# The second block's projection tiles split into high and low parts, and the feed forward's first two tiles multiplied behind its norm

## The reference, cut to what matters

```
h = rmsnorm(x) * (1 + scale) + shift
u = h @ w_in_2[l]                 # 1024 x 2560: 20 tiles of 128 columns
x_lru, gate, q, k, v = split(u)   # 4 tiles each
a = conv -> rg_lru(x_lru) * gelu(gate)
b = diff_attention(rope(q), rope(k), v), then a norm per head
x = x + g1 * (concat(a, b) @ w_out_2[l])
h = rmsnorm(x) * (1 + scale) + shift
x = x + g2 * (swiglu(h) in layer 0, eight routed experts in layer 1)
```

## Time and profile before

| what | us |
|---|---|
| median of 3 runs (2630.61 to 2631.39) | 2630.64 |
| the profiled execution's own time | 2629.47 |
| its span, first to last instruction | 2627.6 |
| TensorE busy | 2565.2 (98%) |
| VectorE busy | 1956.2 (74%) |
| ScalarE busy | 1407.4 (54%) |
| mean granted TensorE clock | 0.99 of full |

### The profile page before, as it was taken

One profiled execution on the slowest core, in us unless ns is written; L12 is line 12 of the kernel. 1 busy time (PEld: TensorE's weight loads), 2 busy tenths in 40 slices (PEclk: granted clock), 3 DMA queues, 4 the chain that ended last, 5 costly groups with the idle time before them and its releaser, 6 DMA issues. The chain is left out here.

```text
span 2627.6 us, 41652 instructions
## 1 busy us (share of the span) xinstructions
PE 2565.2 (98%) x14530; PEld 2221.3 (85%) x14530; DVE 1956.2 (74%) x2656; ACT 1407.4 (54%) x1803; POOL 0.2 (0%) x4
## 2 busy tenths in 40 slices
PE   9999999998999999999999999999999999999998
PEld 5798788897888888898788998878888888888887
DVE  6698358896788777776645654558989889898897
ACT  4653242384544444444434433447777677777775
POOL 0000000000000000000000000000000000000000
PEclk9999999999999999999999999999999999999999
DMA  9422335425788878785434564439999999999996
GB/s 357 149 89 97 128 112 146 148 81 180 241 305 294 297 277 278 257 288 190 140 99 121 183 184 151 138 141 366 352 355 350 349 354 358 350 362 338 365 350 225
DMA packets 223741, 627.11 MB, mean 239 GB/s; under 512 B 15344, under 2 KB 23568, under 8 KB 223376
## 3 DMA queue, kind: packets, MB, share of 16 engines
q1 hardware_dynamic: 223632, 625.64, 68.6%
HBM read 619.29 MB, written 6.29 MB: 238 GB/s over the span
## 5 line engine op out<-in xcount | busy, mean ns | idle before, releaser
L3396 DVE TENSOR_TENSOR wide_low<-wide,wide_high 128x2048 fp32r<-128x2048 f32 x288 | 657.1, 2289 | 98.1 <-ACT wide_high L3271 96.0
L3271 ACT ACTIVATE wide_high<-wide 128x2048 fp32r<-128x2048 f32 x288 | 552.4, 1919 | 197.2 <-PE bank L3124 128.5
L229 DVE TENSOR_TENSOR expert_tile_low<-slot,expert_tile_high 128x1024 fp32r<-128x1024 f32 x216 | 263.8, 1223 | 122.3 <-ACT expert_tile_high L221 118.5
L221 ACT ACTIVATE expert_tile_high<-slot 128x1024 fp32r<-128x1024 f32 x216 | 227.3, 1054 | 182.9 <-PE bank L238 62.7
L3120 PE MATMUL bank<-wide_high,xg_high 128*128 128x512 f32 x768 | 302.8, 394 | 1.2 <-DVE xg_low L3348 1.2
L3121 PE MATMUL bank<-wide_high,xg_low 128*128 128x512 f32 x768 | 299.5, 390 | 0.0
L3124 PE MATMUL bank<-wide_low,xg_high 128*128 128x512 f32 x768 | 205.6, 389 | 0.0
L237 PE MATMUL bank<-h_high,expert_tile_high 128*128 128x256 f32 x704 | 173.4, 284 | 0.0
L238 PE MATMUL bank<-h_low,expert_tile_high 128*128 128x256 f32 x704 | 172.6, 283 | 0.0
L1997 PE MATMUL bank<-expert_tile_high,act_hi 128*128 128x512 f32 x512 | 161.4, 397 | 11.1 <-DVE act_lo L2148 11.1
L3124 PEld LDWEIGHTS bank<-wide_low,xg_high 128*128 128x128 f32 x768 | 144.2, 188 | 30.3
(11 more groups left out here) (537 smaller groups left out, 5035.5 us busy)
## 6 DMA issues: line engine op xcount, KB each, us to landing
wide<-in_moe_gu SPq DMA_DIRECT2D x192, 1024.0 KB, 5.9
wide<-in_moe_d SPq DMA_DIRECT2D x96, 1024.0 KB, 6.2
slot<-in_peer_u SPq DMA_DIRECT2D x128, 512.0 KB, 4.4
slot<-in_peer_v SPq DMA_DIRECT2D x128, 512.0 KB, 4.5
slot<-in_w_in SPq DMA_DIRECT2D x72, 512.0 KB, 3.7
picked_or_ada<-in_ada_w SPq DMA_DIRECT2D x48, 512.0 KB, 5.0
ada_slot<-in_ada_w SPq DMA_DIRECT2D x48, 512.0 KB, 4.6
slot<-in_ffn_gu SPq DMA_DIRECT2D x48, 512.0 KB, 3.6
```

The lines of the kernel that those rows point to most:

```text
L221: core.nc.scalar.activation(self.tile_hi[:, place % 2], core.slot[u][:], ACT.Copy).then_inc(self.hi_ready.sem, 1)
L229: core.nc.vector.tensor_tensor(self.tile_lo[:, place % 2], slot[:], self.tile_hi[:, place % 2].bitcast(F32), ALU.subtract)\
L3271: nc.scalar.activation(w_hi[n % NB][:].rearrange("p c n -> p (c n)"), wide[n % U][:], ACT.Copy).then_inc(hi_ready.sem, 1)
L3396: nc.vector.tensor_tensor(w_lo[n % NB][:].rearrange("p c n -> p (c n)"), wide[n % U][:], w_hi[n % NB][:].rearrange("p c n -> p (c n)").bit ...
```

## The change

1. In both layers the tiles at places 8 to 11 (the middle queries and keys) and 16 to 19 (gelu), and in layer 1 also those at places 2 to 5, are multiplied split instead of whole: 8 tiles in layer 0, 12 in layer 1. The value tiles and the others stay whole.
2. The high parts are made on ScalarE just before `empty(n - 2)`, each waiting for its buffer (two buffers in turn: the high products and the low part of two split tiles earlier). The low parts are made on VectorE at fixed places of its list: tile 8 after the product of gate and convolution, 9 after `soften(0)`, 10 after the next step of the recurrence, 11 after `finish(0)`, 16 after `finish(2)`, 17 to 19 after `finish(3)`. TensorE waits in each split tile between its 16 high and its 8 low products for that low part.
3. The activations are split as well: eight small copies on ScalarE and eight subtractions on VectorE in each layer.
4. SP reloads a buffer as soon as its tile is split, not when it is multiplied.
5. In layer 0 the norm before the feed forward writes the high parts of `h` directly (ScalarE) and the low parts directly (VectorE, one per chunk, among its scalings), and the first two feed forward tiles, split during the output projection, are multiplied chunk by chunk behind it (`pair`). `feed_forward` begins with its third tile.
6. The norm's squares and the position tables use the room of `z` and `att` instead of tiles of their own.

The core of the diff (`...` where lines are left out):

```diff
+    EARLY_SPLIT, MIDDLE_SPLIT = [2, 3, 4, 5] if l == 1 else [], [8, 9, 10, 11]
+    HALVED = EARLY_SPLIT + MIDDLE_SPLIT + [n for n in range(T) if 4 <= ORDER[n] < 8]
...
             for n in range(4, T):
-                sp.wait_ge(used.sem, used.at(n - 3))
+                if n - 4 in HALVED:
+                    sp.wait_ge(low_made.sem, low_made.at(HALVED.index(n - 4) + 1))
...
+            def split_tile(k, out):
+                pe.wait_ge(halver.low_split.sem, halver.low_split.at(C))
+                pe.wait_ge(high_made.sem, high_made.at(k + 1))
+                for c in range(C):
+                    nc.tensor.matmul(out, tile_hi(k)[:, c, :], split.high[:, c, :], start=(c == 0), stop=False)
+                    last = nc.tensor.matmul(out, tile_hi(k)[:, c, :], split.low[:, c, :], start=False, stop=False)
+                last.then_inc(high_used.sem, 1)
+                pe.wait_ge(low_made.sem, low_made.at(k + 1))
+                for c in range(C):
+                    last = nc.tensor.matmul(out, tile_lo(k)[:, c, :], split.high[:, c, :], start=False, stop=(c == C - 1))
+                last.then_inc(used.sem, 1)
...
+            def pair():
+                for c in range(C):
+                    pe.wait_ge(halver.low_split.sem, halver.low_split.at(C + c + 1))
+                    for u in range(2):
...
+            def tile_high(k):
+                n = HALVED[k]
+                u = n % U
+                act.wait_ge(core.landed[u].sem, core.landed[u].at(16 * (n // U + 1)))
+                if previous(k) is not None:
+                    act.wait_ge(high_used.sem, high_used.at(previous(k) + 1))
+                    act.wait_ge(low_made.sem, low_made.at(previous(k) + 1))
+                nc.scalar.activation(tile_hi(k), core.slot[u][:], ACT.Copy).then_inc(high_made.sem, 1)
...
+            def tile_low(k):
+                dve.wait_ge(high_made.sem, high_made.at(k + 1))
+                if previous(k) is not None:
+                    dve.wait_ge(used.sem, used.at(HALVED[previous(k)] + 1))
+                nc.vector.tensor_tensor(tile_lo(k), core.slot[HALVED[k] % U][:], tile_hi(k).bitcast(F32), ALU.subtract).then_inc(low_made.sem, 1)
...
+            tile_lows(8)
             rope(1)
             soften(0)
+            tile_lows(9)
...
+            tile_lows(10)
             rope(2)
             soften(1)
             finish(0)
+            tile_lows(11)
             rope(3)
```

More of the change, by code:

```diff
@@ L2280, with __init__ @@
 class NormParts:
-    def __init__(self, core, ctx, name, x, out, gain, shift, bank):
+    def __init__(self, core, ctx, name, x, out, gain, shift, bank, room, halver=None, split=None, splits=0):
         self.core, self.x, self.out, self.gain, self.shift, self.var = core, x, out, gain, shift, bank[:, 0:N]
-        self.sq = core.sb(ctx, f"{name}_squares", [P, C, N])
+        self.halver, self.split, self.splits = halver, split, splits
+        self.sq = room[:, 0:C, :]
         self.std, self.rstd = (core.sb(ctx, f"{name}_{part}", [P, N]) for part in ("std", "rstd"))
@@ L2304, in vector, with low @@
                 .then_inc(self.scaled.sem, 1)
+            if self.split is not None and c >= 2:
+                self.low(dve, c - 2)
+        if self.split is not None:
+            self.low(dve, C - 2)
+            self.low(dve, C - 1)
+    def low(self, dve, c):
+        nc, split, halver = self.core.nc, self.split, self.halver
+        dve.wait_ge(self.scaled.sem, self.scaled.at(c + 1))
+        dve.wait_ge(halver.moving_split.sem, halver.moving_split.at(self.splits + c + 1))
+        nc.vector.scalar_tensor_tensor(split.low[:, c, :], self.out[:, c, :], self.shift[:, c:c + 1], split.high[:, c, :].bitcast(F32),
+                                       ALU.add, ALU.subtract).then_inc(halver.low_split.sem, 1)
     def squares(self, act, ready=None):
@@ L2516, in passed, with mix_layer @@
             count.passed(k)
-def mix_layer(core, ctx, a, l, x, mods, cos, sin, hide, lam, next_tiles, router):
+def mix_layer(core, ctx, a, l, x, mods, cos, sin, hide, lam, next_tiles, router, split, halver):
     nc = core.nc
@@ L2709, in _ @@
             idle_products(core, 1, 3)
+            if ahead:
+                for u in range(2):
+                    pe.wait_ge(halver.hi_ready.sem, halver.hi_ready.at(u + 1))
+                    pe.wait_ge(halver.lo_ready.sem, halver.lo_ready.at(u + 3))
+                pair()
             if router is not None:
@@ L2843, in _ @@
                 pos.vector(dve)
-            for t in range(T4):
-                convolve(t)
+            if EARLY_SPLIT:
+                activations_low()
+                tile_lows(2, 3)
+            convolve(0)
+            tile_lows(4)
+            convolve(1)
+            tile_lows(5)
+            convolve(2)
+            convolve(3)
             if l == 0:
                 opening.vector_late(dve)
+            if not EARLY_SPLIT:
+                activations_low()
             dve.wait_ge(gated.sem, gated.at(4))
@@ L2889, in _ @@
                                         core.col(f"subln_g{l}", 0), 1.0 - lambda_init(l), ALU.mult, ALU.mult).then_inc(heads_mixed.sem, 1)
+            if ahead:
+                for u in range(2):
+                    halver.lower(dve, u, 0)
             for t in range(C):
@@ L2939, in _, with gate_and_up @@
             zero_banks(core, pe, range(4, 8))
-            pe.wait_ge(halver.low_split.sem, halver.low_split.at(C))
-            with pe.Fori(0, R1) as i:
-                for u in range(U):
+            def gate_and_up(i, start):
+                for u in range(start, U):
                     if u % 2 == 0:
@@ L2958, in silu, with round_ @@
                 nc.scalar.activation(sg[:, w, :], core.bank[2 * w][:, 0:N], ACT.Silu).then_inc(silued.sem, 1)
-            def round_(place, i, before, here):
-                for u in range(U):
+            def round_(place, i, before, here, start=0):
+                for u in range(start, U):
                     halver.high(act, place + u, i)
@@ L3010, in feed_forward @@
     own.passed(FT)
-    halver.passed(U * R, True)
+    halver.passed(U * R, False)
     for u in range(U):
```

123 lines of the change are left out of this document (96 added, 27 removed).

## The result

| | median us | runs |
|---|---|---|
| before | 2630.64 | 5 (2628.24 to 2631.66) |
| after | 2641.98 | 5 (2640.53 to 2643.55) |

The ratio after to before is 1.0042, with a 95% interval of 1.0031 to 1.0053: slower by 11.3 us. The profiled execution of after took 2643.55 us, its span 2641.8.

A forecast was written before the change was run, and what follows sets the result against it. TensorE, busy for 98% of the span, was taken as the bound. Layer 0 +7.3, layer 1 +1.8, the feed forward's start -4.0 and the clock +8.5 gave +13.6 us: 2644 against the median, range 2635 to 2651.

The forecast's parts named there:

- The win per tile: Split tiles in both layers: 2.88 us instead of 3.45, winning 0.57 each, 4.6 in layer 0 and 6.8 in layer 1.
- low parts for places 2 to 5 of layer 1: Layer 1's first tiles: VectorE's added 8.2 us just fits; full 2.3 us win taken, bound 0 to 2 us late.
- The waits: TensorE waits for low parts: tile 8 (layer 0) 3.2 us, tile 9 2.8, tile 11 4.6, tile 16 0.9.
- Small delays on ScalarE: Exponentials and bank emptying behind new ScalarE waits: 0.4 us in layer 0, 0.3 in layer 1.
- The feed forward: From the norm to the third feed forward tile: -4.0 us, bounds -4.5 and -2.0; gap 1.6, clearing 3.4.
- The clock: Behind five new waits in the two layers the clock halves, 1.7 us each: +8.5 us, bounds 0 and 12.5.
- the bound of 1.7 us: Feed forward's start: if the clock falls in the remaining 1.6 us gap, up to 1.7 us goes back.
- Rival A: Same waits in both layers, but the clock holds: +5.1 us, 2636; chance 0.16.
- C: Clock stays low for 5 us each time and falls in the norm too: +19.3 us, 2650; chance 0.2.
- The sum: Whole kernel: +7.3 + 1.8 - 4.0 + 8.5 = +13.6 us, 2644 against the median; chance 0.57.
- Rival B: Low parts come in time in VectorE's list, so waits vanish: 15.4 us won, 2615; chance 0.07.

The follow-up runs named there:

- E2: The changed kernel with all late low parts (tiles 8 to 11, 16, 17) moved earlier in VectorE's list: 2617.95 us, ratio 0.9949 to before.
- E5: The changed kernel with zero matmuls between high and low products of tiles 9, 11 and layer 0's tile 8: 2634.93 us, one run.
- E3: The changed kernel with only tile 11's low part moved, from behind finish(0) to ahead of rope(2): 2631.81 us, one run.
- E6: The changed kernel with only tile 11's low part moved ahead of finish(0), still behind soften(1): 2640.14 us, one run.
- E8: The changed kernel with only tile 9's low part moved, from behind soften(0) to ahead of rope(1): 2637.91 us, one run.
- E4: The changed kernel with no layer tile split, only the feed forward's first two tiles multiplied behind the norm: 2627.79 us, ratio 0.9985 to before.
- E7: E2 with the feed forward's four banks cleared behind the norm's products, replacing idle products there: 2615.03 us, ratio 0.9934 to before.

## Why the prediction was right

**Direction and size.** 2644 was forecast, 2642.0 measured, inside the range, and by the mechanism of the forecast. That the total came so near is in part luck: the clock was put 3.9 us too high, and untouched code, forecast at 0, ran longer in these executions.

**The win per tile.** Without any wait (E2) 8 split tiles win 82.33 - 77.69 = 4.64 us and 12 win 82.33 - 75.39 = 6.94: 0.58 a tile, against 0.57. The rule of the Trainium skill (FP8 and Floating Point Precision, TensorE Precision Notes) on passes would have given an estimate of 0.86 a tile, 17 for 20 tiles; the runs show 11.6. VectorE's low parts for places 2 to 5 of layer 1, which just fitted by the forecast, did fit: no low product there waits.

**The waits.** E5 less E2 is what they cost at full clock: 89.17 - 77.69 = 11.48 in layer 0, forecast 11.5; 83.69 - 75.39 = 8.30 in layer 1, forecast 8.3. They came at the foreseen tiles and at no other. Each stands in the trace 0.3 us shorter than forecast (2.94 for 3.2, 2.5 for 2.8, 4.30 for 4.6, 0.60 for 0.9), because I counted from one start to the next, while the idle time counts from the modelled end of the last record, which is longer than a product's 0.12 us. From start to start layer 0's four are 3.22, 2.79, 4.58 and 0.88 us, 11.47 in all, and that is what the kernel pays. E3, E6 and E8 show the waits of tiles 9 and 11 to be the place in the list: the low part, moved ahead of the steps named as the cause, is no longer late. The low parts of tiles 8 and 16 were moved only together with all others, in E2, where their waits go too.

**Small delays on ScalarE.** I put them at 0.4 and 0.3. By the two sums above nothing is left for them.

**The feed forward.** -4.0 in after and -4.3 alone (E4), against -4.0. The gap was 2.00 us, not 1.6, and the clearing 3.1, not 3.4, so two errors cancelled. In E2 the clock did fall there, the case that the bound of 1.7 us was kept for.

**The clock.** The one term that was mis-sized: 8.5 forecast, 4.64 measured (E5). A fall costs 1.55, close to 1.7; but two of the five waits, tile 8's 2.94 us and layer 1's tile 9 with 2.52, had none behind them in the profiled run. I had taken the three waits of the earlier trace rows as proof that every wait of that size costs the clock. That was one execution's evidence, and two rows speak against it: the first is after's, behind the same L1631 wait of the earlier trace rows (2.82 us there), the second before's own, behind a shorter wait, 2.17 us at L1997, a line that led the list of waits and that the earlier trace rows leave out. The granted clock is 1.00 in both.

```profile
401.12:404.42 3.30, 3.30 (x29) 3.30 (x30) 1.46 (x7) 1.51 (x3) 0.00 (x0) 1.00 0.02 5
```

```profile
801.00:804.00 3.00, 3.00 (x16) 2.46 (x16) 3.00 (x4) 0.48 (x2) 0.00 (x0) 1.00 0.96 363
```

The L1631 wait, 2.7 to 2.9 us in all ten profiles, had a fall right behind it only in that of before. Rival A, no fall at all, was wrong as well, and so was C.

**The sum.** Forecast in full: +13.6. Measured in the touched stretches: +9.92 + 2.92 - 4.0 + 0.4, in all +9.3. Of the difference of 4.3, 3.9 is the clock and 0.7 the small delays, less the 0.4 between the layers, which I had at 0; the little that is left is rounding and the win per tile. The profiled run of after was nevertheless 14.1 us above that of before. The rest, 3.87 + 1.0 = 4.9, lies in untouched code. Of the 3.87, 2.49 are there by the first product of L1121, at 37.58 us in before and 40.07 in after. The clock of after fell 4.0 us earlier in this stretch: the same sixteen products took 1.95 us in before and 3.58 in after.

```profile
33.03 1.95 PE L1089 MATMUL bank<-strip_sum,mod_first_rows 128*128 128x2 f32 x16 [0.81 <-DVE mod_first_rows L970]
```

```profile
33.89 3.58 PE L1089 MATMUL bank<-strip_sum,mod_first_rows 128*128 128x2 f32 x16 [0.79 <-DVE mod_first_rows L970]
```

By the medians the change costs 11.3; what of the 2 us between this and 9.3 is spread of such falls no run here separates.

**Rival B** had asked for the low parts in time, 15.4 us won. I gave it 0.07, rightly for this list; E2, the same instructions in another order, won 12.7, and E7 16.0, with the clearing moved as well.

## What to carry to other kernels

When a second engine prepares an operand in a list of strict order, place that step by when the consumer needs it, ahead of steps that themselves hang on the consumer's newest output; VectorE was busy for only two thirds of these stretches, and that average could not show that TensorE would wait. Before deciding that a split isn't worth it, try it with the producer moved: here the same work went from 0.4% slower to 0.5% faster. Filling such a wait with idle matmuls brings back the clock, not the wait.

## What the runs showed of the hardware that had not been expected

Whether the clock falls behind a wait of 2 to 3 us isn't settled by the length of the wait. Layer 0's tile 8 waited 2.94, 2.94, 2.93 and 2.93 us in after, E3, E6 and E8. The rows of the stretch right behind it, in E3 and then in E8:

```profile
1309.30:1312.60 3.30, 3.30 (x12) 2.67 (x12) 0.34 (x1) 2.27 (x4) 0.00 (x0) 0.50 0.73 230
```

```profile
1309.30:1312.60 3.30, 3.28 (x21) 2.54 (x22) 2.82 (x4) 3.06 (x4) 0.00 (x0) 1.00 0.72 210
```

The same instructions, 12 matmuls in one and 21 in the other: E3 and E6 ran at 1.2 GHz there, 6.8 us in all, from 0.9 us before the wait ended, while after and E8 kept 2.4. In the same way layer 1's tile 9 waited 2.52 in three kernels: the clock held in after and E6 and fell in E3. The 2.00 us gap in front of the pair held in after, E3, E5, E6 and E8 and fell in E2. After the four waits of 4.3 us in after and E8 it fell each time, and so it did at every wait of 3.07 us or more in the ten profiles, 25 of them. Under that length the place matters as well: in all ten profiles a wait of 2.2 to 2.4 us at L1997 near 800 us held the clock, and one of 2.2 to 2.5 us at the same line near 900 us lost it. What decides is open. The Trainium skill (TensorE: Matmul & The Clock Gate, Part 1: The HAM clock gate) says that the chip watches activity in a window that runs freely and does not start with the kernel, so that the same instructions can meet it at another phase; that would fit the tiles that differ from run to run, but nothing here shows the phase. A forecast should price a wait of 2 to 3 us as a chance of a fall, not as a fall.
